# Shifted rows of a depthwise convolution copied inside on-chip memory instead of through a scratch tensor in device memory

## The chip, the cores and the metric

One Trainium2 chip, all 8 of its cores, each running the same program on its own share of the tokens, with no exchange between cores. The metric is device time in microseconds (us) of the slowest core, less being better. A run of the kernel before is shown three times (below), and one further execution was profiled.

## The reference, cut to what matters

One decoder layer on x of (2, 8192, 1024) float32:

```python
x = x + 0.5 * swiglu(rmsnorm(x, ffn1_norm), w_gate, w_up, w_down)          # FFN 1, hidden 2816
h = rmsnorm(x, mix_norm)
glu_a, glu_b, q, k, v, g_conv, g_attn = split(h @ w_in)
u = glu_a * sigmoid(glu_b)                                                  # 1024 channels
c = causal_depthwise_conv(u, dw_w, dw_b)        # out[t] = sum_k w[k] * u[t - 30 + k], width 31
c = silu(layernorm(c)) @ conv_w_proj
a = sliding_window_gqa_sinks(rope(q), rope(k), v, sinks) @ attn_w_o         # window 128
x = x + (sigmoid(g_conv + b1) * c + sigmoid(g_attn + b2) * a) @ w_out
x = x + 0.5 * swiglu(rmsnorm(x, ffn2_norm), ...)                            # FFN 2
out = rmsnorm(x, final_norm)
```

The part that changes is how the gated inputs `u` get to the causal convolution: every output needs the 30 tokens in front of it.

## The kernel before, in words

Each core has 2048 tokens and a halo of 128 tokens in front, as four tiles of 512 tokens (NT). Channels lie on the 128 partitions, in 8 chunks, and tokens along the free dimension. A tile goes through FFN 1 (`f_a`), the mixer (`m_norm`, `m_rest`) and FFN 2 (`f_b`). The mixer of tile t is interleaved with FFN 2 of tile t-1 and FFN 1 of tile t+1, so that TensorE has FFN matmuls (`ps<-xnF,wt`, `ps<-Hh,wt`) to run between those of the mixer (`ps<-xnM,wt`).

The convolution stage of a tile stands at the start of `m_rest` (L854). For the 8 channel chunks cc, in a software pipeline: `glu(cc)` (L724) makes the gated chunk, `u_in(cc)` (L739) follows one step behind, `conv(cc)` (L746) three steps behind. `glu` runs two projections of 8 matmuls of 512 columns, a tanh on ACT (ScalarE), and one scalar_tensor_tensor on DVE (VectorE), which writes the tile `uT`, of three buffers. A DMA on the queue of SP (SyncE) then writes `uT` to the scratch tensor `ush` in device memory. `u_in` reads it back with 4 DMAs into `RR`, a tile of four buffers. `RR` has partition 32*k + c holding channel c shifted by k tokens, for k of 0 to 3, and the four groups g of 32 channels side by side. So `conv` contracts 4 taps at a time over the 128 partitions: 8 tap groups times 4 channel groups is 32 matmuls of a 128x32 weight and 512 columns (`ps<-RR,wt`), read at the free offset 4*j. A DVE tensor_scalar then moves the result to `cvo`. In tile 0 `glu` is also run over the 128 halo tokens (matmuls `ps<-S,wt` of 128 columns, the gated halo in a part of `S` named `uh`), and this goes to `ush` by a DMA of its own (`ush<-S`). In later tiles the 31 columns in front of a tile are in `ush` already.

Weights come through nine slots `wt`, shared by everything. The first read of a block is float32, from `wall` or `wd`, by a DMA on POOL's queue (GpSimd). The block is stored once as bf16 in `wac` or `wdc` (`wac<-wt`), and later reads are `wt<-wac` and `wt<-wdc`. The stores and the cached reads are issued on SP's queue, in between the DMAs of the convolution. SP issues in program order, and an instruction that waits for a semaphore holds back all that stands behind it.

What sets the order: `Plan.schedule` (L185) places the recorded tasks on the engines by estimated durations and by keys. `Plan.dma` (L178) gives a DMA task an estimated issue time of 0.1 us per DMA, and `t` as the time to landing. `Stream` (L230) decides when weight loads and stores are issued. Those estimates set only the order. The waits are made from true dependencies (`_deps`, L62): `u_in` waits for the writes of `ush` and, from the fifth chunk on, for the convolution that last read the same `RR` buffer. `glu` waits, for its `uT` buffer, for the DMA that last read it.

Helpers record every compute instruction, so most rows name L82 (`emit_op`), L98 (`emit_dma`) or L508 (`MMW`), and the tiles tell them apart.

Of the kernel before, what the change touches and what calls it, by code (L numbers as in the profile page):

```python
# [15 lines left out]
RW = 28 + NT  # L16
# [119 lines left out]
class Plan:  # L136
# [32 lines left out]
    def op(self, eng, fn, rd=(), wr=(), t=None, use=None):  # L169
        k = self._task(eng)  # L170
        k.ops.append((0, fn, tuple(rd), tuple(wr), use))
        k.t += eng.typ if t is None else t
        if use is not None and use not in k.uses:
            k.uses.append(use)
            use.left += 1
        self._link(k, rd, wr)

    def dma(self, q, dsem, moves, rd=(), wr=(), t=5.0):  # L178
        k = self._task(q)
        k.ops.append((1, dsem, tuple(rd), tuple(wr), moves))  # L180
# [168 lines left out]
def build_nc():  # L349
    nc = bass.Bass("TRN2", target_bir_lowering=False)  # L350
    dt = nc.dram_tensor
# [9 lines left out]
    outT_d = dt("outT", [D, TOK], F32, kind="ExternalOutput").ap()  # L361
    wac_d = dt("wac", [NBLK_A, 128, 2048], BF16, kind="Internal").ap()
    wdc_d = dt("wdc", [32, 128, 11 * 128], BF16, kind="Internal").ap()
    ush_d = dt("ush", [8, 128, TL], BF16, kind="Internal").ap()

    with ExitStack() as es:
        def sb(name, shape, dtype):
            return es.enter_context(nc.sbuf_tensor(name, shape, dtype))

        def mksem(name):  # L370
            return Sem(es.enter_context(nc.semaphore(name)))
# [12 lines left out]
        def bufs(n):  # L384
            return [Buf() for _ in range(n)]
# [3 lines left out]
        xnM = sb("xnM", [128, 8, NT], BF16); xnM_b = bufs(8)  # L389
# [3 lines left out]
        qa = sb("qa", [128, 8, NT], BF16); qa_b = [[Buf() for _ in range(4)] for _ in range(8)]  # L393
        kT = sb("kT", [128, 2, 640], BF16); kT_b = [[Buf(), Buf()] for _ in range(2)]
        V = sb("V", [128, 5, 256], BF16); V_b = bufs(5)
        uT = sb("uT", [128, 3, NT], BF16); uT_b = bufs(3)
        NRR = 4
        RR = [sb(f"RR{i}", [128, 4, RW], BF16) for i in range(NRR)]; RR_b = bufs(NRR)
        RR_s = [mksem(f"s_rr{i}") for i in range(NRR)]
        ush_b = bufs(8); ush_s = [mksem(f"s_ush{i}") for i in range(3)]  # L400
        NW = 9
        wt = [sb(f"wt{i}", [128, 2048], BF16) for i in range(NW)]; wt_b = bufs(NW)
        wt_s = [mksem(f"s_wt{i}") for i in range(NW)]
# [7 lines left out]
        S = sb("S", [128, 8, 132], F32); S_b = bufs(2)  # L411
# [16 lines left out]
        xnh = S[:].rearrange("p a b -> p (a b)")[:, 0:512].bitcast(BF16).rearrange("p (a b) -> p a b", a=8); xnh_b = bufs(8)  # L428
# [4 lines left out]
        s_x = [mksem(f"s_x{i}") for i in range(8)]  # L433
        s_xh = mksem("s_xh")
        s_pos = [mksem(f"s_pos{i}") for i in range(2)]
        ushh_b = bufs(8); ushh_s = [mksem(f"s_ushh{i}") for i in range(2)]
        uh = S[:].rearrange("p a b -> p (a b)")[:, 768:896].bitcast(BF16).rearrange("p (a b) -> p a b", a=2); uh_b = bufs(2)
        s_out = [mksem(f"s_out{i}") for i in range(8)]

        ps = [es.enter_context(nc.psum_tensor(f"ps{i}", [128, NT], F32)) for i in range(3)]  # L440
# [37 lines left out]
        SA = SD = Stream(chan, POOL, SP, wview, wt_b, wt_s, wt_ss, wt_hs, wsrc, wcache, [8.0] * 3 + [18.0 + 2.0 * i for i in range(NW - 3)],  # L478
                         {"A": (3.6, 1.6, 1.7), "D": (2.5, 1.1, 1.2), "W": (1.8, 0.8, 0.85)}, (X_b[0][5],))
        alias(cvo_b, Xh_b + Hhh_b + [accH[1]])  # L480
        alias(S_b, xnh_b + uh_b + [cosh_b, sinh_b])

        def ACTF(out, in_, func, rd, wr, t=None, **kw):
            op(ACT, partial(act, out=out, in_=in_, func=func, **kw), rd, wr, t)

        def STT(out, in0, scalar, in1, op0, op1, rd, wr, t=None):
            op(DVE, partial(stt, out=out, in0=in0, scalar=scalar, in1=in1, op0=op0, op1=op1), rd, wr, t)
# [13 lines left out]
        def COPY(out, in_, rd, wr, t=None):  # L501
            op(DVE, partial(nc.vector.tensor_copy, out=out, in_=in_), rd, wr, t)
# [4 lines left out]
        def MMW(out, use, pick, rhs, start, stop, rd, wr, t=None):  # L507
            op(PE, lambda: mm(out, lhsT=pick(use.slot), rhs=rhs, start=start, stop=stop), rd, wr, t, use)  # L508

        def load_x(t, after=()):  # L510
            b0 = HALO + t * NT
            for c in range(8):
                dma(ACT if t == 0 and c % 2 else SP, s_x[c], [(X[t % 2][:, c, :], xT_d[128 * c:128 * c + 128, b0:b0 + NT])],
                    rd=after, wr=(X_b[t % 2][c],), t=7.0)

        def proj(pst, pb, use, sub, rhs_t, rhs_bufs, N):
            G.join(True)
            for kc in range(8):
                MMW(pst[:, 0:N], use, lambda s, kc=kc: s[:, kc, sub * 128:(sub + 1) * 128], rhs_t[:, kc, 0:N], kc == 0, kc == 7,
                    rhs_bufs[kc] if isinstance(rhs_bufs[kc], list) else [rhs_bufs[kc]], (pb,), t=N / 2360)  # L520
            G.join(False)

# [566 lines left out]
```

How the kernel before makes its waits and increments, by code:

```python
    def wait(self, sem, val):  # L40
        if val <= 0:
            return
        if sem is self.sem:
            if val > sem.n or not SAME_ENGINE_SYNC or self.no_self:
                return
        if self.known.get(sem, 0) >= val:
            return
        self.e.wait_ge(sem.h, val)
        self.known[sem] = val
# [29 lines left out]
def emit_op(eng, fn, rd=(), wr=()):  # L79
    for s, v in _deps(rd, wr, eng.sem).items():
        eng.wait(s, v)
    inst = fn()
    eng.sem.n += 1
    inst.then_inc(eng.sem.h, 1)
    ev = eng.sem.n
    for b in wr:
        b.w = {eng.sem: ev}
        b.r = {}
    for b in rd:
        if b.r.get(eng.sem, 0) < ev:
            b.r[eng.sem] = ev
# [1 line left out]
def emit_dma(q, dsem, moves, rd=(), wr=()):  # L93
    for s, v in _deps(rd, wr, None).items():
        q.wait(s, v)
    q.wait(dsem, dsem.n)
    for out_ap, in_ap in moves:
        q.e.dma_start(out=out_ap, in_=in_ap).then_inc(dsem.h, 16)
        dsem.n += 16
    for b in wr:
        b.w = {dsem: dsem.n}
        b.r = {}
    for b in rd:
        b.r[dsem] = dsem.n
```

## Time and profile before

| what | us |
|---|---|
| three runs | 1957.9, 1786.03, 1765.64 (median 1786.03) |
| the profiled execution's own time | 1768.82 |
| its span, from first to last instruction (slowest core, core 5) | 1767.8 |
| spans of the 8 cores | 1748.8 to 1767.8 |
| TensorE (PE) busy | 1638.3 (93% of the span) |
| VectorE (DVE), ScalarE (ACT), GpSimd (POOL) busy | 704.0, 651.8, 687.7 |

How to read it: busy is time in which the engine ran an instruction. PE is matmuls, PEld the loading of weights into the array. Queue rows (SPq) are the issuing of DMAs and are not counted as busy. In a timeline row the first number is the start and the second the duration of a merged run of x instructions; what stands in brackets is how long the engine idled before it, and what ended that. The granted clock is TensorE's, as a share of full speed.

### The profile page before, as it was taken

Reading aid. Unit: us, or ns where it says so; the run is one execution under the profiler, and the core shown is the slowest. Engines: PE = TensorE matmul, PEld = TensorE weight load, DVE = VectorE, ACT = ScalarE, POOL = GpSimd, SP = SyncE. Lnnn points to the kernel's source line nnn. Section 1 sums busy time; section 2 is a strip of 40 time slices with the busy share of each in tenths; the row PEclk is TensorE's granted clock in tenths of the full one; section 3 lists DMA queues with packets and bytes.
Section 4 is the critical chain, followed back from the end, with each engine's and each line's share of the span. In section 5 each row is a group of like instructions: output and inputs, shape, how many; then the busy total and the mean of one; then the engine's idle time right before and its main releaser. Section 6 shows DMA issues by size and latency. Waiting matters only on the chain.

```text
span 1767.8 us, 29593 instructions; the slowest of 8 cores (1748.8 to 1767.8 us)
## 1 busy us (share of the span) xinstructions
PE 1638.3 (93%) x9060; PEld 739.0 (42%) x9060; DVE 704.0 (40%) x1180; ACT 651.8 (37%) x1396; POOL 687.7 (39%) x723
## 2 busy tenths in 40 slices
PE   6999677899988899989999999999998999998996
PEld 2555333344433334434443344444443444443442
DVE  3432422764243365441225266542224356524212
ACT  3212312664132366443222257553222258422221
POOL 1014023865332595413331387423322277413232
PEclk9999788999999999999999999999999999999998
DMA  8998987579999999985556978764443953443542
GB/s 171 197 217 167 208 204 178 140 190 183 203 196 239 233 180 172 192 274 156 163 147 176 238 198 190 194 240 152 142 138 115 237 199 98 145 152 128 182 123 81
DMA packets 118121, 315.39 MB, mean 178 GB/s; under 512 B 14544, under 2 KB 36304, under 8 KB 117968
## 3 DMA queue, kind: packets, MB, share of 16 engines
q1 hardware_dynamic: 92480, 231.46, 41.8%
q0 software_dynamic: 24768, 80.95, 29.0%
q8 instruction: 78, 1.28, 0.3%
q10 hardware_dynamic: 720, 1.09, 0.2%
q14 instruction: 75, 0.61, 0.1%
HBM read 327.01 MB, written 67.37 MB: 223 GB/s over the span
## 4 chain that ended last, share of the span: by engine, by line
PE 80%; DMA 11%; issue 2%; ACT 2%; DVE 2%; SPq 2%; POOL 1%; ACTq 0%; DVEq 0%; POOLq 0%
PE ps L508 74%; PE ps L82 5%; DMA RR<-ush 3%; DMA ush<-S 3%; DMA ush<-uT 2%; SPq L98 2%; DMA X<-xT 1%; DMA wt<-wall 1%; PE ps L706 1%; DMA outT<-tf 1%; ACT ps L82 0%; POOL acc L82 0%; DVE xnF L82 0%; DVE S L82 0%; ACT S L82 0%
## 5 line engine op out<-in xcount | busy, mean ns | idle before, releaser
L508 PE MATMUL ps<-xnF,wt 128*128 128x512 bf16 x2816 | 652.1, 386 | 15.9 <-DVE xnF L82 6.5
L508 PEld LDWEIGHTS ps<-xnF,wt 128*128 128x128 bf16 x2816 | 270.0, 99 | 357.2 <-issue 64.3
L508 PE MATMUL ps<-Hh,wt 128*128 128x512 bf16 x1408 | 328.6, 380 | 0.0
L508 PE MATMUL ps<-xnM,wt 128*128 128x512 bf16 x1344 | 310.9, 383 | 0.4 <-DVE xnM L82 0.2
L82 ACT ACTIVATE tf<-ps 128x512 f32<-128x512 f32 x304 | 179.9, 595 | 312.5 <-PE ps L508 291.0
L82 POOL TENSOR_TENSOR Hh<-tf 128x512 bf16<-128x512 f32 x128 | 164.7, 1287 | 187.9 <-PE ps L508 115.1
L82 DVE SCALAR_TENSOR_TENSOR tf<-tf,ps 128x512 f32<-128x512 f32 x176 | 120.4, 684 | 260.8 <-PE ps L508 248.0
L508 PEld LDWEIGHTS ps<-Hh,wt 128*128 128x128 bf16 x1408 | 134.3, 98 | 160.8 <-issue 9.3
L508 PEld LDWEIGHTS ps<-xnM,wt 128*128 128x128 bf16 x1344 | 129.9, 98 | 169.7 <-issue 22.2
L98 POOL DMA_DIRECT2D wt<-wall x121 | 67.7, 563 | 245.6 <-PE ps L508 214.5
L82 DVE SCALAR_TENSOR_TENSOR X<-ps,X 128x512 f32<-128x512 f32 x96 | 66.3, 691 | 199.5 <-PE ps L508 197.5
L82 ACT ACTIVATE S<-S,sm 128x129 f32<-128x129 f32 x256 | 103.6, 405 | 65.8 <-DVE sm L82 47.5
L82 DVE SCALAR_TENSOR_TENSOR tm<-tm,ps 128x512 f32<-128x512 f32 (+1 forms) x86 | 50.2, 585 | 168.9 <-PE ps L508 150.1
L508 PE MATMUL ps<-RR,wt 128*32 128x512 bf16 x1024 | 72.2, 431 | 40.9 <-DMA RR<-ush 40.8
L82 POOL TENSOR_TENSOR acc<-acc,tf 128x512 f32<-128x512 f32 x56 | 70.9, 1266 | 91.5 <-ACT tf L82 91.3
L82 POOL TENSOR_TENSOR cvo<-tm 128x512 bf16<-128x512 f32 x32 | 40.5, 1265 | 157.0 <-DVE tm L82 157.0
L508 PE MATMUL ps<-cvo,wt 128*128 128x512 bf16 (+1 forms) x432 | 97.0, 314 | 0.8 <-POOL cvo L82 0.8
L82 POOL TENSOR_TENSOR acc<-acc,tm 128x512 f32<-128x512 f32 x56 | 70.8, 1264 | 66.4 <-ACT tm L82 66.1
L82 POOL TENSOR_TENSOR P<-S,sm 128x512 bf16<-128x512 f32 x64 | 67.3, 1051 | 68.7 <-DVE sm L82 24.5
L82 POOL TENSOR_TENSOR cvo<-cvo,acc 128x512 f32<-128x512 f32 x64 | 83.4, 1307 | 14.6 <-ACT acc L82 13.3
L82 ACT ACTIVATE tm<-cvo 128x512 f32<-128x512 f32 (+1 forms) x67 | 39.7, 595 | 133.2 <-DVE cvo L82 131.5
L82 ACT ACTIVATE tm<-ps,hcols_sb 128x512 f32<-128x512 f32 x64 | 43.6, 688 | 113.3 <-PE ps L508 108.4
(97 smaller groups left out, 1471.8 us busy)
## 6 DMA issues: line engine op xcount, KB each, us to landing
wt<-wac SPq DMA_DIRECT2D x207, 512.0 KB, 4.8
wt<-wall POOLq DMA_DIRECT2D x121, 512.0 KB, 9.7
wac<-wt SPq DMA_DIRECT2D x82, 512.0 KB, 8.7
wt<-wdc SPq DMA_DIRECT2D x80, 352.0 KB, 3.1
RR<-ush SPq DMA_DIRECT2D x128, 135.0 KB, 6.3
wt<-wd POOLq DMA_DIRECT2D x48, 352.0 KB, 7.1
wdc<-wt SPq DMA_DIRECT2D x32, 352.0 KB, 5.8
X<-xT SPq DMA_DIRECT2D x28, 256.0 KB, 10.8
```

Source lines behind the costliest of these rows:

```text
L82: inst = fn()
L98: q.e.dma_start(out=out_ap, in_=in_ap).then_inc(dsem.h, 16)
L508: op(PE, lambda: mm(out, lhsT=pick(use.slot), rhs=rhs, start=start, stop=stop), rd, wr, t, use)
L706: op(PE, lambda kc=kc: mm(pst[:, 0:256], lhsT=xn_t[:, kc, c0:c0 + 128], rhs=uv.slot[:, kc, 0:256], start=(kc == 0), stop=(kc == 7)), (xn_b ...
```

## The change

The gated chunk no longer goes to device memory. `uT` grows to 32 + 512 columns: columns 0 to 30 are the 31 tokens in front of the tile, 31 to 542 the tile's own. In tile 0 the front columns come from a `glu` over the last 31 halo tokens alone (matmuls of 31 columns instead of 128). In later tiles a DVE copy brings them from a new tile `past`, and every `glu` ends with a DVE copy that saves its last 31 columns there. `u_in` is now 16 DMAs instead of 4, one for each pair of shift k and channel group g, each from 32 partitions of `uT` to 32 partitions of `RR`. The tensor `ush`, its buffers and its semaphores, and the `uh` part of `S` are gone. The plan's estimate of issue time is 0.35 us per DMA for tasks of 8 and more DMAs.

```diff
@@ class Plan, dma
-        k.t = 0.1 * len(moves)
+        k.t = (0.1 if len(moves) < 8 else 0.35) * len(moves)
@@ build_nc
-    ush_d = dt("ush", [8, 128, TL], BF16, kind="Internal").ap()
...
-        uT = sb("uT", [128, 3, NT], BF16); uT_b = bufs(3)
+        uT = sb("uT", [128, 3, 32 + NT], BF16); uT_b = bufs(3)
+        past = sb("past", [128, 8, 32], BF16); past_b = bufs(8)
...
-        ush_b = bufs(8); ush_s = [mksem(f"s_ush{i}") for i in range(3)]
...
-        def proj(pst, pb, use, sub, rhs_t, rhs_bufs, N):
+        def proj(pst, pb, use, sub, rhs_t, rhs_bufs, N, c0=0):
             G.join(True)
             for kc in range(8):
-                MMW(pst[:, 0:N], use, lambda s, kc=kc: s[:, kc, sub * 128:(sub + 1) * 128], rhs_t[:, kc, 0:N], kc == 0, kc == 7,
+                MMW(pst[:, 0:N], use, lambda s, kc=kc: s[:, kc, sub * 128:(sub + 1) * 128], rhs_t[:, kc, c0:c0 + N], kc == 0, kc == 7,
...
         def glu(cc, base, halo):
             use = SA.use(("A", 28 + cc), "M")
-            parts = [(xnM, xnM_b, NT, uT[:, cc % 3, :], uT_b[cc % 3], base, ush_s[cc % 3], ush_b[cc])]
+            u_t, u_b = uT[:, cc % 3, :], uT_b[cc % 3]
+            parts = [(xnM, xnM_b, 0, NT, u_t[:, 31:31 + NT])]
             if halo:
-                parts.append((xnh, xnh_b, HALO, uh[:, cc % 2, :], uh_b[cc % 2], 0, ushh_s[cc % 2], ushh_b[cc]))
-            for xn_t, xn_bufs, N, u_t, u_b, c0, sem, db in parts:
+                parts.append((xnh, xnh_b, HALO - 31, 31, u_t[:, 0:31]))
+            else:
+                COPY(u_t[:, 0:31], past[:, cc, 0:31], (past_b[cc],), (u_b,), 0.15)
+            for xn_t, xn_bufs, c0, N, dst in parts:
...
-                STT(u_t, t_t[:, 0:N], 1.0, pa[:, 0:N], ALU.add, ALU.mult, (t_b, pab), (u_b,))
-                dma(SP, sem, [(ush_d[cc][:, c0:c0 + N], u_t)], rd=(u_b,), wr=(db,), t=6.0)
+                STT(dst, t_t[:, 0:N], 1.0, pa[:, 0:N], ALU.add, ALU.mult, (t_b, pab), (u_b,), t=0.15 + 0.55 * N / 512)
+            COPY(past[:, cc, 0:31], u_t[:, NT:NT + 31], (u_b,), (past_b[cc],), 0.15)
 
         def u_in(cc, base):
-            dma(SP, RR_s[cc % NRR], [(RR[cc % NRR][32 * k:32 * k + 32, :, :],
-                                      ush_d[cc][:, base - 31 + k:base - 31 + k + RW].rearrange("(g c) t -> c g t", g=4)) for k in range(4)],
-                rd=(ush_b[cc], ushh_b[cc]), wr=(RR_b[cc % NRR],), t=8.0)
+            dma(SP, RR_s[cc % NRR], [(RR[cc % NRR][32 * k:32 * k + 32, g, :], uT[32 * g:32 * g + 32, cc % 3, k:k + RW])
+                                     for k in range(4) for g in range(4)], rd=(uT_b[cc % 3],), wr=(RR_b[cc % NRR],), t=6.0)
```

SP's queue in the convolution stage of the last tile (tile 3), the first chunks, before the change. `ush<-uT` is the write of a gated chunk, `RR0<-ush ... x4` the read of its shifted rows, `wt<-wac` a cached weight load:

```order
L98 DMA ush<-uT 128x512
L98 DMA wt0<-wac 128x2048
L98 DMA wt7<-wac 128x2048
L98 DMA ush<-uT 128x512
L98 DMA wt8<-wac 128x2048
L98 DMA RR0<-ush 32x4x540 x4
L98 DMA ush<-uT 128x512
L98 DMA wt2<-wac 128x2048
L98 DMA RR1<-ush 32x4x540 x4
```

The same place after the change:

```order
L98 DMA RR0<-uT 32x540 x16
L98 DMA wt3<-wac 128x2048
L98 DMA RR1<-uT 32x540 x16
L98 DMA wt6<-wac 128x2048
L98 DMA wt4<-wac 128x2048
L98 DMA wt5<-wac 128x2048
L98 DMA RR2<-uT 32x540 x16
L98 DMA wt0<-wac 128x2048
L98 DMA RR3<-uT 32x540 x16
```

The write and the read of a chunk became one block of 16 DMAs, and each block stands as a whole ahead of the next weight load. Over the stage, 8 writes and 32 reads became 128 copies, with ten weight loads between the first block and the last.

TensorE's queue at the first convolution of tile 3, before. `ps<-xnM` with wt5 are the last of the gating projections of the first four chunks, `ps<-xnF` FFN matmuls, `ps<-RR0` the convolution of chunk 0:

```order
L508 MATMUL ps7<-xnM,wt5 128x512 x8
L508 MATMUL ps2<-xnF,wt6 128x512 x8
L508 MATMUL ps0<-xnF,wt4 128x512 x8
L508 MATMUL ps1<-xnF,wt4 128x512 x8
L508 MATMUL ps2<-xnF,wt0 128x512 x8
L508 MATMUL ps34<-RR0,wt7 32x512 x32
L508 MATMUL ps6<-xnM,wt8 128x512 x8
```

And after:

```order
L505 MATMUL ps7<-xnM,wt2 128x512 x8
L505 MATMUL ps2<-xnF,wt7 128x512 x8
L505 MATMUL ps0<-xnF,wt1 128x512 x8
L505 MATMUL ps34<-RR0,wt8 32x512 x32
L505 MATMUL ps6<-xnM,wt3 128x512 x8
```

Of the four groups of 8 FFN matmuls ahead of the first convolution two are left; the other two stand later, behind the stage. In tile 2 it is the same. In tile 1 the stage has as many FFN matmuls as before, and in tile 0 one group of 8 fewer.

## Rows read from the trace of the kernel before

**Rows 1.** The page: span, busy time of TensorE.

```profile
span 1767.8 us, 29593 instructions; the slowest of 8 cores (1748.8 to 1767.8 us)
PE 1638.3 (93%) x9060; PEld 739.0 (42%) x9060; DVE 704.0 (40%) x1180; ACT 651.8 (37%) x1396; POOL 687.7 (39%) x723
```

**Rows 2.** Waits of TensorE: who waited for whom, us in total, times, longest.

```profile
PE ps L508 <- DMA RR<-ush: 40.8, 11, 11.8
PE ps L508 <- DMA wt<-wac: 5.2, 1, 5.2
```

**Rows 3.** Busy time by stretch: the convolution stages of tiles 0 to 3.

```profile
core 5: us, PE busy (x) PEld busy (x) DVE busy (x) ACT busy (x) POOL busy (x), PEclk, DMA share, GB/s
183.00:293.00 110.00, 79.82 (x602) 37.01 (x601) 30.79 (x55) 22.12 (x38) 21.78 (x25) 0.84 0.92 209
530.00:600.00 70.00, 58.08 (x420) 24.15 (x421) 20.54 (x32) 13.64 (x22) 18.80 (x20) 0.90 0.97 234
959.00:1019.00 60.00, 56.69 (x433) 24.14 (x435) 20.23 (x31) 13.63 (x22) 15.69 (x14) 0.97 0.96 231
1364.00:1420.00 56.00, 54.94 (x425) 23.48 (x427) 19.56 (x30) 13.95 (x23) 16.21 (x13) 1.00 0.96 243
```

**Rows 4.** Timeline of TensorE, convolutions of tile 0: the third last and the last.

```profile
263.16 3.32 PE L508 MATMUL ps<-RR,wt 128*32 128x512 bf16 x32 [2.83 <-DMA RR<-ush]
...
289.83 3.60 PE L508 MATMUL ps<-RR,wt 128*32 128x512 bf16 x32 [11.79 <-DMA RR<-ush]
```

**Rows 5.** Timeline of SP's queue, tile 0.

```profile
190.27 0.32 SPq L98 DMA_DIRECT2D ush<-uT  x1
...
193.22 0.43 SPq L98 DMA_DIRECT2D ush<-S  x1
...
209.69 1.75 SPq L98 DMA_DIRECT2D RR<-ush  x4
```

**Rows 6.** Timeline of SP's queue: the first gated chunk of tiles 1, 2 and 3.

```profile
530.15 1.77 SPq L98 DMA_DIRECT2D ush<-uT  x2
...
959.26 0.32 SPq L98 DMA_DIRECT2D ush<-uT  x1
...
1364.28 0.32 SPq L98 DMA_DIRECT2D ush<-uT  x1
1364.74 0.82 SPq L98 DMA_DIRECT2D wt<-wac  x2
```

**Rows 7.** Timeline of TensorE: last convolutions of tiles 1 to 3, an FFN group before.

```profile
599.72 1.91 PE L508 MATMUL ps<-RR,wt 128*32 128x512 bf16 x32 [0.45 <-DMA RR<-ush]
...
1018.11 1.91 PE L508 MATMUL ps<-RR,wt 128*32 128x512 bf16 x32
...
1373.53 7.07 PE L508 MATMUL ps<-xnF,wt 128*128 128x512 bf16 x32
...
1419.52 1.91 PE L508 MATMUL ps<-RR,wt 128*32 128x512 bf16 x32
```

**Rows 8.** Timeline of SP's queue, tile 3: two of its eight groups of 4 reads.

```profile
1368.67 1.76 SPq L98 DMA_DIRECT2D RR<-ush  x4
...
1372.16 3.38 SPq L98 DMA_DIRECT2D RR<-ush  x4
```

**Rows 9.** Issues on SP's queue by kind: duration ns min/median/max.

```profile
L98 SPq DMA_DIRECT2D wt<-wac x207: 319/320/1626, 188.6 to 1683.1; - x104
L98 SPq DMA_DIRECT2D RR<-ush x128: 302/429/1958, 209.7 to 1413.3; - x128
L98 SPq DMA_DIRECT2D cvo<-xT x1: 942/942/942, 5.1 to 5.1; - x1
```

**Rows 10.** Reads of tile 3 (RR<-ush, 1360 to 1420): from issue to landing.

```profile
DMA to landing us min/median/max: 3.2/6.1/9.7
```

**Rows 11.** Groups by line and shape: halo matmuls, a small DVE instruction.

```profile
L508 PE MATMUL ps<-S,wt 128*128 128x128 bf16 x496 | 33.1, 219 | 1.2 <-ACT tm L82 1.2
L82 DVE RECIPROCAL sm<-sm 128x4 f32<-128x4 f32 x64 | 11.0, 172 | 31.9 <-ACT S L82 31.7
```

More of the change, by code:

```diff
@@ L435, in build_nc @@
         s_pos = [mksem(f"s_pos{i}") for i in range(2)]
-        ushh_b = bufs(8); ushh_s = [mksem(f"s_ushh{i}") for i in range(2)]
-        uh = S[:].rearrange("p a b -> p (a b)")[:, 768:896].bitcast(BF16).rearrange("p (a b) -> p a b", a=2); uh_b = bufs(2)
         s_out = [mksem(f"s_out{i}") for i in range(8)]
@@ L480, in build_nc @@
         alias(cvo_b, Xh_b + Hhh_b + [accH[1]])
-        alias(S_b, xnh_b + uh_b + [cosh_b, sinh_b])
+        alias(S_b, xnh_b + [cosh_b, sinh_b])
         def ACTF(out, in_, func, rd, wr, t=None, **kw):
@@ L725, in glu @@
             use = SA.use(("A", 28 + cc), "M")
-            parts = [(xnM, xnM_b, NT, uT[:, cc % 3, :], uT_b[cc % 3], base, ush_s[cc % 3], ush_b[cc])]
+            u_t, u_b = uT[:, cc % 3, :], uT_b[cc % 3]
+            parts = [(xnM, xnM_b, 0, NT, u_t[:, 31:31 + NT])]
             if halo:
-                parts.append((xnh, xnh_b, HALO, uh[:, cc % 2, :], uh_b[cc % 2], 0, ushh_s[cc % 2], ushh_b[cc]))
-            for xn_t, xn_bufs, N, u_t, u_b, c0, sem, db in parts:
+                parts.append((xnh, xnh_b, HALO - 31, 31, u_t[:, 0:31]))
+            else:
+                COPY(u_t[:, 0:31], past[:, cc, 0:31], (past_b[cc],), (u_b,), 0.15)
+            for xn_t, xn_bufs, c0, N, dst in parts:
                 pa, pab = bM5.get()
                 pb_, pbb = bM5.get()
-                proj(pb_, pbb, use, 1, xn_t, xn_bufs, N)
+                proj(pb_, pbb, use, 1, xn_t, xn_bufs, N, c0)
                 t_t, t_b = tmM.get()
-                ACTF(t_t[:, 0:N], pb_[:, 0:N], AF.Tanh, (pbb,), (t_b,), scale=0.5)
-                proj(pa, pab, use, 0, xn_t, xn_bufs, N)
-                STT(u_t, t_t[:, 0:N], 1.0, pa[:, 0:N], ALU.add, ALU.mult, (t_b, pab), (u_b,))
-                dma(SP, sem, [(ush_d[cc][:, c0:c0 + N], u_t)], rd=(u_b,), wr=(db,), t=6.0)
+                ACTF(t_t[:, 0:N], pb_[:, 0:N], AF.Tanh, (pbb,), (t_b,), t=0.2 + 0.4 * N / 512, scale=0.5)
+                proj(pa, pab, use, 0, xn_t, xn_bufs, N, c0)
+                STT(dst, t_t[:, 0:N], 1.0, pa[:, 0:N], ALU.add, ALU.mult, (t_b, pab), (u_b,), t=0.15 + 0.55 * N / 512)
+            COPY(past[:, cc, 0:31], u_t[:, NT:NT + 31], (u_b,), (past_b[cc],), 0.15)
         def u_in(cc, base):
-            dma(SP, RR_s[cc % NRR], [(RR[cc % NRR][32 * k:32 * k + 32, :, :],
-                                      ush_d[cc][:, base - 31 + k:base - 31 + k + RW].rearrange("(g c) t -> c g t", g=4)) for k in range(4)],
-                rd=(ush_b[cc], ushh_b[cc]), wr=(RR_b[cc % NRR],), t=8.0)
+            dma(SP, RR_s[cc % NRR], [(RR[cc % NRR][32 * k:32 * k + 32, g, :], uT[32 * g:32 * g + 32, cc % 3, k:k + RW])
+                                     for k in range(4) for g in range(4)], rd=(uT_b[cc % 3],), wr=(RR_b[cc % NRR],), t=6.0)
         taps = [None]
```

## The prediction

> **What bounds the kernel now.** I read the page first: TensorE is busy 1638.3 of 1767.8 us [rows 1]. The kernel is bound by it, so an edit counts only through the 129.5 us in which TensorE stands, or by making it stand more. Then TensorE's waits: the largest is for the shifted rows, 40.8 us in 11 waits, and one wait of 5.2 us for a cached weight load [rows 2]. Then the four convolution stages one by one [rows 3]: TensorE is busy 79.8 of 110 us in tile 0, 58.1 of 70 in tile 1, 56.7 of 60 in tile 2 and 54.9 of 56 in tile 3. So the wait to be removed sits almost wholly in the first two tiles. In tiles 2 and 3 there is next to nothing to win. Behind a long wait TensorE also runs slower for a few us: the 32 matmuls of a convolution take 1.91 us at full clock and 3.3 to 3.6 behind waits of 2.8 and 11.8 us [rows 4, 7], and the granted clock of the stage is 0.84 in tile 0 against 1.00 in tile 3 [rows 3]. That is some 1.7 us for each of the seven or so long waits, 12 us. All that could be won is thus 40.8 + 5.2 + 12 = 58 us.
>
> **Why it waits.** The path of a chunk is: gating on DVE, write to `ush`, landing, read into `RR`, landing, convolution. SP stands at the wait for the write before it may issue the read, with everything behind it: in tile 0 the halo write goes out at 193.2 and the reads only at 209.7 [rows 5]. The change takes out one of the two landings and this stop.
>
> **What it adds.** SP now issues 128 copies of 34.6 KB (32 partitions x 540 x 2 bytes) per tile, in blocks of 16, in place of 8 writes and 32 reads (in tile 0 also 8 halo writes). The trace has no copy of 32 partitions and none within on-chip memory, so its issue is bounded from both sides. Low end: a load behind a pause takes 0.32 us [rows 9], 16 of them 5.1. High end: the eight groups of 4 reads of tile 3 take 16.7 us together, from about 1.7 to 3.38 each (two of the eight in [rows 8]), which is 0.52 per read and 8.3 per block. Between them lies the plain group of 4 in 1.76 us, 0.44 each, 7.0 for 16. This is the nearest row, since such a read, too, goes to blocks of 32 partitions in rows of 540 elements, and 429 ns is the median of all 128 [rows 9]. I take it. With 0.14 us of waiting in front of a block (0.46 from one issue to the next less 0.32 for the issue itself [rows 6]) a block is 7.2 us.
>
> The Trainium skill, page "DMA: Bandwidth & Descriptors", section "Why a DMA increments its semaphore by 16 and not by 1", gives a plain copy 512 cycles of the issuing sequencer in the older generation, data transfer not counted. At the 1.2 GHz of the SyncEngine ("Trainium Kernel Development and Optimization", NeuronCore Architecture) that is an estimate of 0.43 us whatever the size, and speaks against four times as many DMAs. By it a block would be 6.9 us; a cost that shrank with the size would bring it to the low end. The 429 ns of the reads agree with it, the 320 ns of loads behind a pause do not.
>
> **Does SP keep up?** While TensorE runs densely, a chunk is 16 gating matmuls and one convolution. 32 FFN matmuls take 7.07 us [rows 7], so 16 take 3.5, and with 1.9 that makes 5.4 us per chunk, against 7.2 plus the weight loads on SP. The queue of SP therefore becomes what sets the end of the stage. That end is when the last convolution starts: first gated chunk, plus 8 x 7.2 = 57.6, plus the other issues between the blocks at 0.46 each, plus the last landing. A read of tile 3 lands after 3.2 us at least and 6.1 in the median [rows 10], under bursts of four 138 KB reads; I take 4.5.
> - Tile 3: first chunk 1364.3 [rows 6]. Ten weight loads, 4.6. 1364.3 + 57.6 + 4.6 + 4.5 = 1431.0. Before it was 1419.5 [rows 7]; 16 FFN matmuls fewer stand ahead of it, so like is compared with 1416.0. Loss 15.0.
> - Tile 2: 959.3 + 57.6 + 5.1 (eleven issues) + 4.5 = 1026.5, against 1018.1 - 3.5 = 1014.6. Loss 11.9.
> - Tile 1: 530.2 + 57.6 + 5.1 + 4.5 = 597.4 against 599.7 [rows 7]. Gain 2.3.
> - Tile 0: the chunk is written at 190.3 [rows 5], with its front columns at about 192. 192 + 57.6 + 3.7 + 6.1 (the median landing, as this is the stage full of float32 weight loads) = 259.4, against 289.8 [rows 4] less 1.8 for 8 FFN matmuls. That would be 28.6 won. The DMA engines are 92% busy there for 110 us [rows 3], 101 us of work, of which only the writes, some 4 us, go. Weights loaded ahead give slack, but hardly 28 us; I take 20, with 12 and 28 as ends.
>
> Sum: 15.0 + 11.9 - 2.3 - 20 = +4.6 us on the profiled execution's 1768.8: 1773 us. (The median of the three runs shown, 1786, lies 17 above that execution and their lowest 3 below; I forecast on the scale of the profiled one.)
>
> **Small terms.** The 56 new DVE copies of 31 columns cost about as much as the smallest DVE instruction, 0.17 us [rows 11]: 14 in a tile, 2.4 us, while DVE is busy only 20 of 60 us of a stage [rows 3]; hidden. If DVE were full they would cost 9.6 us in all. The copy into `uT` waits until the block of three chunks earlier has landed, and behind it on DVE stand the gating, the moving of a finished convolution to `cvo` and the FFN's products, which free TensorE's banks. The convolution next on TensorE waits for the same landing, so I put it at 0, with at most 1.4 us (two DVE instructions) on each of 16 chunks, 22 us, as the other end. The halo's 128 matmuls shrink from 128 to 31 columns: at 33.1 us for 496 [rows 11] all of them are 8.5 us and at most 6.5 could go; SP paces tile 0, so 0. Weight loads behind a block go out up to 7 us later; they are planned ahead, 0.
>
> **The rivals.**
> 1. Issue is cheap: 0.32 us per copy, a block of 5.3. Then SP keeps pace with TensorE. Tile 3 comes out even, tile 2 wins its waits (3), tile 1 its 12 and one slow restart (13), tile 0 28: 44 us, 1725 us. For it: every load behind a pause, and the first read of a group, takes this. Against: reads in a row don't. Half way, at 0.37, it is 28 us, 1741.
> 2. Slower: SP's queue is held up as it was between the reads. The place is the 128 back-to-back issues of each tile, the price 0.52 per copy, 8.5 us per block, 10.4 us more per tile. Tile 3 loses 25.4, tile 2 22.3, tile 1 8.1, and tile 0 wins 12: +44, 1813 us. One us on a block is worth 8 us in each of four tiles, 32, so the time passes 2% (35 us) from a block of 8.2 us, 0.50 per copy. For it: 3.38 us for four reads in the quietest tile [rows 8]. Against: a block spreads the same bytes over 7 us instead of under 2, which leaves the queues emptier.
> 3. The landing of float32 weights holds SP in tile 0, so the one tile that should win gives only 4 us: 1789.
>
> **How the numbers follow.** A measurement of this kernel can tell about 2% from no change. Forecast 0.52 (1750 to 1800). Rival 1 0.20, of which 0.13 lies beyond 2% (under 1733) and the rest between 0.32 and 0.37 per copy. Rival 2 0.23. Rival 3 0.05. So faster 0.13, same 0.64, slower 0.23. The range takes in the cheap issue almost to its end and all of rival 2: 1728 to 1818.
>
> **What would show it.** Right: SP's row for the new copies has a median near 0.43 us and blocks of about 7 us; TensorE's waits for `RR` shrink in tile 0, stay in tile 1, and appear in tiles 2 and 3 as a series of short waits of 2 us, with the last convolution of tile 3 about 67 us behind the first gated chunk. Wrong: a median of 0.32 and blocks under 6 us; or waits of TensorE that name DVE or `wt`; or tile 0 with as long a stage as before.

## Result, and the profile after

The changed kernel took 1880.04, 1881.23 and 1962.45 us (median 1881.23) against a median of 1786.03 before: a ratio of 1.061 [1.053, 1.068], slower by 6%. Some executions, of either kernel, show a lower granted clock on the cores of one die and take longer (1962.45 here, 1957.9 before); ratios, and the medians of the kernel before that stand under Experiments, leave them out. The profiled execution took 1880.04 us, against 1768.82. The forecast was 1773, range 1728 to 1818; the result lies outside it, on the side of the second rival.

The page of the kernel after (slowest core, core 6): the span, the busy times, the chain of work that ended last by engine, the costliest group of the convolution (count | busy us, mean ns | idle before it and its releaser), and the row of the new copies among the DMA issues (count, KB each, median us from issue to landing).

```profile
span 1879.0 us, 29979 instructions; the slowest of 8 cores (1860.7 to 1879.0 us)
...
PE 1662.0 (88%) x9060; PEld 743.5 (40%) x9060; DVE 710.0 (38%) x1236; ACT 650.3 (35%) x1396; POOL 689.5 (37%) x723
...
PE 70%; SPq 17%; DMA 5%; issue 3%; DVE 2%; ACT 2%; POOL 1%; ACTq 0%; DVEq 0%; POOLq 0%
...
L505 PE MATMUL ps<-RR,wt 128*32 128x512 bf16 x1024 | 94.8, 535 | 126.2 <-DMA RR<-uT 95.9
...
RR<-uT SPq DMA_DIRECT2D x512, 33.8 KB, 2.3
```

The same three rows of the kernel before, the chain, the convolution and the DMA that fills `RR`:

```profile
PE 80%; DMA 11%; issue 2%; ACT 2%; DVE 2%; SPq 2%; POOL 1%; ACTq 0%; DVEq 0%; POOLq 0%
L508 PE MATMUL ps<-RR,wt 128*32 128x512 bf16 x1024 | 72.2, 431 | 40.9 <-DMA RR<-ush 40.8
RR<-ush SPq DMA_DIRECT2D x128, 135.0 KB, 6.3
```

The span grew by 111.2 us. TensorE's busy time grew by 23.7 of them [rows 1], though it runs fewer columns: the 1024 convolution matmuls take 535 ns each in place of 431. The rest is idle time, 217.0 us against 129.5. A sixth of the chain (17%, before 2%) is now SP's queue, that is, an engine that computes nothing. The copies themselves are quick: from issue to landing 2.3 us in the median.

TensorE's waits after (us in total, times, longest), and SP's issues (duration in ns, least/median/most; first and last start):

```profile
PE ps L505 <- DMA RR<-uT: 95.9, 20, 8.2
...
PE ps L505 <- DVE uT L82: 30.2, 7, 7.0
...
PE ps L505 <- DMA wt<-wac: 4.0, 5, 2.3
```

```profile
L98 SPq DMA_DIRECT2D RR<-uT x512: 507/591/1966, 190.4 to 1525.0; - x171
L98 SPq DMA_DIRECT2D wt<-wac x207: 319/320/1100, 185.5 to 1794.1; - x104
```

The wait for the shifted rows, 40.8 us in 11 waits before [rows 2], is 95.9 in 20. And an issue of the new copies holds SP for 591 ns in the median and never under 507, where a read of `ush` took 429 [rows 9]. The loads of weights, on the same queue among them, still take 320.

The four convolution stages in windows (busy us of PE, PEld, DVE, ACT, POOL with the instruction counts, then the granted clock, the DMA engines' busy share, GB/s), to be held against [rows 3]:

```profile
183.00:288.00 105.00, 73.80 (x562) 31.70 (x565) 30.72 (x64) 20.67 (x37) 21.33 (x24) 0.82 0.76 176
535.00:631.00 96.00, 56.88 (x402) 22.91 (x399) 19.46 (x40) 12.42 (x20) 18.77 (x19) 0.80 0.67 170
985.00:1088.00 103.00, 72.09 (x471) 29.72 (x470) 28.72 (x57) 15.12 (x25) 16.09 (x14) 0.87 0.42 112
1434.00:1530.00 96.00, 66.01 (x442) 26.75 (x440) 22.00 (x43) 13.62 (x22) 16.20 (x13) 0.86 0.37 108
```

All four stages now look alike: from the first block to the start of the last convolution they take 92 to 101 us, where they took 55 to 100 before. TensorE's granted clock in them is 0.80 to 0.87. In tiles 2 and 3 the DMA engines are busy only 0.42 and 0.37 of the time (0.96 before), and TensorE waits all the same. What paces the stage is thus not the transfer. SP's timeline in the stage of tile 3 (start, duration; merged runs), with the first blocks of tiles 1 and 2 ahead of it, shows what does:

```profile
527.20 10.40 SPq L98 DMA_DIRECT2D RR<-uT  x16
...
992.16 10.30 SPq L98 DMA_DIRECT2D RR<-uT  x16
...
1435.29 10.99 SPq L98 DMA_DIRECT2D RR<-uT  x16
1446.43 0.48 SPq L98 DMA_DIRECT2D wt<-wac  x1
1447.05 10.23 SPq L98 DMA_DIRECT2D RR<-uT  x16
1457.42 1.43 SPq L98 DMA_DIRECT2D wt<-wac  x3
1459.00 10.15 SPq L98 DMA_DIRECT2D RR<-uT  x16
...
1514.98 10.60 SPq L98 DMA_DIRECT2D RR<-uT  x16
```

The queue has no gap: block, weight loads, block. A block takes 10.0 to 11.1 us, the eight together 83.3, so 10.4 each; within a block one copy follows the other by 0.63 us in the median. Three last convolutions, those of tiles 0 to 2, and then three convolutions of tile 3 (in brackets the idle time before, and its releaser):

```profile
287.61 1.91 PE L505 MATMUL ps<-RR,wt 128*32 128x512 bf16 x32
...
628.01 3.60 PE L505 MATMUL ps<-RR,wt 128*32 128x512 bf16 x32 [8.00 <-DMA RR<-uT]
...
1084.23 3.28 PE L505 MATMUL ps<-RR,wt 128*32 128x512 bf16 x32 [3.63 <-DMA RR<-uT]
...
1458.80 3.36 PE L505 MATMUL ps<-RR,wt 128*32 128x512 bf16 x32 [4.98 <-DMA RR<-uT]
...
1470.76 3.60 PE L505 MATMUL ps<-RR,wt 128*32 128x512 bf16 x32 [4.84 <-DVE uT L82]
...
1527.00 3.60 PE L505 MATMUL ps<-RR,wt 128*32 128x512 bf16 x32 [5.39 <-DMA RR<-uT]
```

A convolution starts 1 to 2 us behind the end of its block (block 1459.00 to 1469.15, convolution 1470.76; last block to 1525.58, convolution 1527.00). Before it TensorE has idled for 3.6 to 5.4 us in five of the eight chunks of tile 3, and behind that idling its 32 matmuls take 3.1 to 3.6 us in place of 1.91, little more than half the rate. Over the four tiles 22 of the 32 convolutions are slow in this way, against 7 before. That is the 22.6 us by which the convolution's busy time grew (94.8 against 72.2).

Some of these waits are put down to a DVE copy. DVE at that time:

```profile
1470.50 0.18 DVE L82 COPY uT<-past 128x31 bf16<-128x31 bf16 x1 [7.42 <-DMA RR<-uT]
1470.78 0.69 DVE L82 SCALAR_TENSOR_TENSOR uT<-tm,ps 128x512 bf16<-128x512 f32 x1
```

That copy had itself been waiting for a landing, began at 1470.50 and ended 0.08 us before the convolution. In tile 3 the two convolutions whose wait names DVE start 1.6 and 1.7 us behind the end of their block, the other six 1.4 to 1.8. So the copy is not the cause but work of a second engine that the same landing lets go.

### The profile page after: what moved, and what is told of

It is laid out like the page before. It is cut to its first block, busy times and chain, and to the rows that moved or that the text cites. A ratio compares the mean times of both kernels' runs of the same rounds, so it can differ in the third digit from the quotient of the medians.

```text
span 1879.0 us, 29979 instructions; the slowest of 8 cores (1860.7 to 1879.0 us)
## 1 busy us (share of the span) xinstructions
PE 1662.0 (88%) x9060; PEld 743.5 (40%) x9060; DVE 710.0 (38%) x1236; ACT 650.3 (35%) x1396; POOL 689.5 (37%) x723
## 4 chain that ended last, share of the span: by engine, by line
PE 70%; SPq 17%; DMA 5%; issue 3%; DVE 2%; ACT 2%; POOL 1%; ACTq 0%; DVEq 0%; POOLq 0%
PE ps L505 64%; SPq L98 17%; PE ps L82 5%; DMA X<-xT 2%; DMA RR<-uT 1%; DMA outT<-tf 1%; PE ps L703 1%; DVE xnF L82 0%; ACT ps L82 0%; POOL acc L82 0%; DVE tf L82 0%; DVE tm L82 0%; ACT L82 0%; POOL P L82 0%; ACT sx L82 0%
## 5 line engine op out<-in xcount | busy, mean ns | idle before, releaser
L505 PE MATMUL ps<-RR,wt 128*32 128x512 bf16 x1024 | 94.8, 535 | 126.2 <-DMA RR<-uT 95.9
L82 ACT ACTIVATE tm<-cvo 128x512 f32<-128x512 f32 (+1 forms) x67 | 39.3, 592 | 218.0 <-DVE cvo L82 217.0
L505 PEld LDWEIGHTS ps<-RR,wt 128*32 128x32 bf16 x1024 | 35.6, 123 | 175.6 <-issue 168.5
L82 POOL TENSOR_TENSOR acc<-acc,cvo 128x512 f32<-128x512 f32 x24 | 30.4, 1265 | 192.9 <-DVE cvo L82 192.9
## 6 DMA issues: line engine op xcount, KB each, us to landing
RR<-uT SPq DMA_DIRECT2D x512, 33.8 KB, 2.3
```

The source lines that it names most:

```text
L82: inst = fn()
```

## Experiments

Two theories of the price of an issue stood against each other. A: an issue whose source is on the chip takes SP 0.59 us, whatever its size. B: it is the shape, 32 partitions and one row of 1080 bytes each, or the small size. The rest is about what follows from the price: is it SP's queue that sets the time, or the places that the plan's estimate gives the blocks; and would another engine or queue do the work for less? Where no median is given, the kernel ran once. The kernel before was run again beside them: its median was 1769.28 us beside the 16 reads from device memory, the copies over 128 partitions, the four copies and the split with ACT; 1768.08 beside the copies of 32 columns, the write in four, the estimate of 0.62 and the 16 copies on DVE; and 1770.66 beside the other four. The diffs are shortened, and `n` in them is `cc % NRR`.

### The kernel before, with 16 reads of the small shape

```diff
-  k.t = 0.1 * len(moves)
+  k.t = (0.1 if len(moves) < 8 else 0.35) * len(moves)
...
-  (RR[n][32*k:32*k+32, :, :], ush_d[cc][:, base-31+k:base-31+k+RW].rearrange("(g c) t -> c g t", g=4)) for k in range(4)
+  (RR[n][32*k:32*k+32, g, :], ush_d[cc][32*g:32*g+32, base-31+k:base-31+k+RW]) for k in range(4) for g in range(4)
```

> The kernel before, still through ush in device memory, but with the 16 reads of 32 partitions x 540 columns per chunk in place of 4, and the plan's 0.35 us for them. Theory A (a copy from on-chip memory to on-chip memory costs SP more than one from device memory): an issue stays near 0.43 us (median), a block of 16 near 7 us, and the time is some 1800 to 1830 us. Theory B (a copy of 32 partitions costs 0.59 us whatever its source, or the number is all that counts): median 0.59 us, blocks of 10 us, and the time is above the changed kernel's 1880, some 1900 us, as the landing of the write comes on top.

Measured: 1846.24 us. SP's issues and TensorE's waits:

```profile
L98 SPq DMA_DIRECT2D RR<-ush x512: 302/422/2006, 206.0 to 1504.5; - x171
```

```profile
PE ps L508 <- DMA RR<-ush: 43.2, 12, 9.5
PE ps L508 <- DMA wt<-wac: 36.5, 13, 6.2
```

The same number of copies of the same shape costs 422 ns each when the source is in device memory; the blocks of tile 3 take 7.3 to 8.7 us. So the shape is not what costs 591. But the time lies 16 us above the range expected under A: the count is dear even at 422 ns. With the write and its landing kept, 16 issues in place of 4 and the plan's 0.35 for them, this kernel is 77 us slower than before. TensorE idles 34.6 us more, most of it for weights (36.5 against 5.2), whose loads stand behind the blocks on the same queue, and is busy for 42.8 us more (1681.1 against 1638.3).

### 16 copies over all 128 partitions

```diff
-  (RR[n][32*k:32*k+32, g, :], uT[32*g:32*g+32, cc % 3, k:k+RW]) for k in range(4) for g in range(4)
+  (RR[n][:, g, 135*j:135*j+135], uT[:, cc % 3, 135*j:135*j+135]) for j in range(4) for g in range(4)
```

> The changed kernel with 16 copies of 128 partitions x 135 columns per chunk (same number, same bytes, on-chip to on-chip, but without the move across partitions, so the convolution reads unshifted data). Theory A (on-chip source is dear): median issue again 0.55 to 0.6 us and a time near 1880. Theory B (the 32-partition shape is dear): issue back at 0.43 us, blocks of 7 us, time near 1790 to 1810. More and shorter descriptors per copy could raise the issue on their own; then it is above 0.6.

Measured: 1892.44 us.

```profile
L98 SPq DMA_DIRECT2D RR<-uT x512: 464/601/4042, 187.8 to 1537.6; - x171
```

The same bytes over 128 partitions cost as much. B falls for the partitions. (This kernel leaves out the move across partitions, and is a measure of time only.)

### 16 copies of 32 columns

```diff
-  (RR[n][32*k:32*k+32, g, :], uT[32*g:32*g+32, cc % 3, k:k+RW])
+  (RR[n][32*k:32*k+32, g, 0:32], uT[32*g:32*g+32, cc % 3, k:k+32])
```

> The changed kernel with 16 copies of 32 partitions x 32 columns per chunk instead of 540 (it leaves out the other 508 columns; RR is set to 0 once at the start). If the issue of an on-chip copy costs a fixed time whatever its size: median again 0.59 us, blocks of 10 us, and the time is within 15 us of the changed kernel's 1880. If transfer, landing or queues that fill up hold the issue back: median under 0.45 us and a time under 1800.

Measured: 1879.08 us, with copies of 2.0 KB.

```profile
L98 SPq DMA_DIRECT2D RR<-uT x512: 507/591/1593, 189.2 to 1526.2; - x171
```

A seventeenth of the bytes changes neither the issue (591) nor the time (1880.04; the copies leave out 508 of 540 columns). The transfer has no part in the loss.

### The kernel before, its write to `ush` in four DMAs

```diff
-  (ush_d[cc][:, c0:c0+N], u_t)
+  (ush_d[cc][:, c0+i*N//4:c0+(i+1)*N//4], u_t[:, i*N//4:(i+1)*N//4]) for i in range(4)
```

> The kernel before with each write of a gated chunk to ush as 4 DMAs of 128 columns (on-chip to device memory), to see issues of that direction one behind the other. If it is the on-chip source that makes an issue dear, they take 0.59 us in a row; if it is that both ends lie on chip, they take 0.42 as the reads from device memory do. The time is 1770 to 1790 us either way (96 more issues, 40 to 60 us on SP, most of it under waits it has anyway).

Measured: 1774.59 us.

```profile
L98 SPq DMA_DIRECT2D ush<-uT x128: 319/434/4517, 191.1 to 1411.1; - x128
```

From the chip to device memory an issue costs 434 ns, back to back, with `uT` as the source. Theory A as first put, an on-chip source, is thus too wide: it is a source and a destination that are both on the chip.

### Four copies of 128 partitions and 540 columns

```diff
+  (RR[n][:, g, :], uT[:, cc % 3, g:g+RW]) for g in range(4)
```

> The changed kernel with 4 copies of 128 partitions x 540 columns per chunk, on-chip to on-chip (same bytes, a quarter of the copies; it leaves out the move across partitions, the shift is by g instead of k). If the number of issues on SP's queue is what costs 6 per cent: blocks of 2.5 us at most, waits of TensorE for RR under 15 us in all, and 1725 to 1750 us, below the kernel before. If on-chip to on-chip transfer or the DVE copies into uT are the cause, it stays above 1800.

Measured: 1721.72 us, the fastest of all runs and 3 below what was expected; issues of 464/586/2977 ns. TensorE's waits, and SP's timeline in tile 3:

```profile
PE ps L505 <- DVE uT L82: 9.1, 1, 9.1
PE ps L505 <- DMA RR<-uT: 7.1, 1, 7.1
```

```profile
1336.49 2.37 SPq L98 DMA_DIRECT2D RR<-uT  x4
1341.82 2.35 SPq L98 DMA_DIRECT2D RR<-uT  x4
```

The same bytes move within the chip and the price per issue is the same, but there are four issues to a chunk, 2.4 us. Now SP waits for TensorE (a block each 5.4 us, the pace that the prediction worked out for it), and the whole gain that the idea promised is there: 48 us below the kernel before. Taking out the scratch tensor is good; the 12 further issues to a chunk, with the places that the plan gives the blocks (it counts a block here as 0.4 us, and as 5.6 us with 16 copies), cost 158 us. No run parts the two at four copies. This arrangement does not place shift k and channel group g as the convolution needs them, so it is a measure and not a way out.

### Eight copies of 64 partitions

```diff
+  (RR[n][64*h:64*h+64, g, :], uT[64*h:64*h+64, cc % 3, g:g+RW]) for h in range(2) for g in range(4)
```

> The changed kernel with 8 copies of 64 partitions x 540 columns per chunk (same bytes, on-chip to on-chip, half the number; it leaves out the move across partitions). The plan gives 0.35 us per copy, as for 16. Each issue stays at 0.59 us and a block takes 5.0 us, which with the weight loads is just about TensorE's 5.4 us per chunk. If the count of issues times 0.63 us against TensorE's pace is the whole mechanism, the loss is gone at this point, not halved: 1720 to 1750 us, close to the 1722 of four copies. If it goes by the count alone, it is half way between four and sixteen, 1790 to 1810.

Measured: 1768.21 us; issues of 461/597/3048 ns, waits for `RR` 26.5 us in 8.

```profile
1366.63 4.94 SPq L98 DMA_DIRECT2D RR<-uT  x8
1371.72 0.48 SPq L98 DMA_DIRECT2D wt<-wac  x1
1372.35 4.95 SPq L98 DMA_DIRECT2D RR<-uT  x8
```

Of the 158 us between four and sixteen copies 46 are left at eight. Neither expectation was met. From the first block of tile 3 (1354.17) to the last (1397.45) a chunk takes 6.2 us on SP, weight loads included, against TensorE's 5.4. Eight copies stand just beyond the point where SP's queue becomes the bound, so most of the loss is gone and some is left. This kernel too leaves out the move across partitions.

### The plan's estimate at the measured price

```diff
-  k.t = (0.1 if len(moves) < 8 else 0.35) * len(moves)
+  k.t = (0.1 if len(moves) < 8 else 0.62) * len(moves)
```

> The changed kernel with the plan's estimate for a task of 16 copies raised from 0.35 to 0.62 us each, the distance that the trace of the changed kernel shows; nothing else. If the damage came only from convolutions standing too early in TensorE's order, the plan now puts FFN matmuls between them: waits for RR fall below 40 us and the time to 1770 to 1810 us, with SP's blocks still 10 us long. If SP's queue is the bound in itself (it also carries the weight loads), the waits only move to weights and to the end of the stage: 1840 to 1880.

Measured: median 1850.91, ratio 1.043 [1.040, 1.045].

```profile
PE ps L505 <- DMA wt<-wac: 48.5, 16, 7.3
...
PE ps L505 <- DMA RR<-uT: 14.8, 4, 7.3
```

With the true price in the plan, TensorE waits little for `RR`, and for weights in its place: a load that stands behind a block comes late. The order is worth some 30 us. The remaining 4% goes with the queue: in tile 3 SP has no gap here either, with blocks of 9.8 to 10.7 us and 21 weight loads between the first and the last, 12.0 us per chunk.

### The plan's estimate at 0.1 for every DMA

```diff
+  k.t = 0.1 * len(moves)
```

> The changed kernel with the plan's old estimate, 0.1 us per DMA, for the 16 copies too; nothing else. Convolutions then stand as close behind one another as before. If SP's queue is the bound, their wait only grows by what FFN work is taken out from between: 1875 to 1910 us. If the order that 0.35 us gives was itself a part of the loss, it is under 1860.

Measured: 1934.18 us; waits for `RR` 93.9 us in 17, and 54.4 in 10 that name the DVE copy. The worse the estimate, the later the work: 0.62 gives 1851, 0.35 gives 1880, 0.1 gives 1934. The last, a single run, lies 24 us above what was expected, so the order matters more than I had put it at.

### Half of the copies on ACT's queue

```diff
-  k.t = (0.1 if len(moves) < 8 else 0.35) * len(moves)
+  k.t = (0.1 if len(moves) < 8 else 0.6) * len(moves)
...
-  dma(SP, RR_s[n], [... for k in range(4) for g in range(4)], ...)
+  for q, sems, bufs_, ks in ((SP, RR_s, RR_b, (0, 1)), (ACT, RR_s2, RR_b2, (2, 3))):
+      dma(q, sems[n], [... for k in ks for g in range(4)], ...)
```

> The changed kernel with the 16 copies of a chunk split: shifts 0 and 1 issued by SP, shifts 2 and 3 by ACT, each with its own semaphores; the plan gives 0.6 us per copy. The result is the reference's. If SP's queue is the bound: 8 issues take 5 us, less than TensorE's 5.4 us per chunk, waits for RR shrink to under 30 us and the time falls to 1745 to 1790 us. ACT gets 8 x 8 x 4 issues of 0.6 us, 154 us, and if it delays the tanh and the exponentials behind it, 1790 to 1830. If the issue is slow because both queues share one descriptor generator, each issue becomes about 1.2 us and nothing is won: 1870 to 1890.

Measured: median 1762.0, ratio 0.995 [0.990, 0.999].

```profile
L98 SPq DMA_DIRECT2D RR<-uT x256: 507/598/2401, 190.2 to 1397.3; - x128
L98 ACTq DMA_DIRECT2D RR<-uT x256: 514/619/2252, 193.6 to 1395.7; - x128
```

Both queues pay the price, and it does not double, as the third case of the expectation had it: they issue side by side, SP's at 598 ns against 591 alone. TensorE's waits for `RR` fall to 10.2 us in 5 (and 11.4 in 3 that name the DVE copy). Half the issues on each queue, with 0.6 in the plan, bring back the 6%, and not more. The estimate alone gave 1851 above, so the second queue is worth some 89 us of the 118.

### The 16 copies on DVE

```diff
-  k.t = (0.1 if len(moves) < 8 else 0.35) * len(moves)
+  k.t = (0.1 if len(moves) < 8 else 0.62) * len(moves)
...
-  dma(SP, RR_s[n], [...])
+  for k in range(4):
+      for g in range(4):
+          COPY(RR[n][32*k:32*k+32, g, :], uT[32*g:32*g+32, cc % 3, k:k+RW], (uT_b[cc % 3],), (RR_b3[n][4*k+g],), 0.25)
```

> The 16 copies of a chunk made by DVE (32 partitions x 540 columns, from one block of 32 partitions to another) instead of by DMA; SP issues none of them and there is no landing. The result is the reference's. If such a copy costs 0.2 to 0.3 us (bf16, in on-chip memory): DVE gets 512 of them, 100 to 150 us more, still under 60% busy, the waits of TensorE in the stages all but go, and the time is 1715 to 1745 us, as with four copies. If it costs 0.55 us or more, as DVE's float32 instructions of 512 columns do, a stage needs 70 us of DVE for the copies alone beside 20 for the rest, and the time is over 1820.

Measured: median 1799.73, ratio 1.020 [1.014, 1.026]. The costliest group of the page, DVE's timeline, POOL's, and a window of tile 3 (columns as above):

```profile
L82 DVE COPY RR<-uT 32x540 bf16<-32x540 bf16 x512 | 191.7, 374 | 15.1
```

```profile
1390.96 5.16 DVE L82 COPY RR<-uT 32x540 bf16<-32x540 bf16 x16
...
1398.00 7.08 DVE L82 COPY RR<-uT 32x540 bf16<-32x540 bf16 x16
```

```profile
1398.35 1.39 POOL L82 TENSOR_TENSOR acc<-cvo 128x512 f32<-128x512 f32 x1 [43.85 <-PE ps L506]
1399.69 1.32 POOL L82 TENSOR_TENSOR acc<-acc,tm 128x512 f32<-128x512 f32 x1
```

```profile
1385.00:1442.00 57.00, 41.30 (x323) 16.58 (x324) 52.35 (x128) 10.13 (x17) 13.26 (x11) 0.88 0.25 84
```

Half the copies take under 0.3 us (median 294 ns), but the mean is 374. The block beside no POOL work takes 5.16 us, the one beside two tensor_tensors 7.08. Of all 512 copies 40 took over 1 us, 1.25 to 1.79, and each of the 40 overlapped a POOL tensor_tensor and ended 0.15 to 0.17 us behind its end; of the 468 under 0.4 us only 18 touched one, by 0.25 us at most. The Trainium skill, page "SBUF — State Buffer", section "SBUF: two separate sides", says that GpSimd and VectorE, where VectorE runs in a two-port mode or has two inputs in on-chip memory, take one shared pair of ports as an exclusive lock for the whole instruction. These rows agree with it; in which mode the copies ran no run shows. The expectation had two cases, about 0.25 and 0.55 and more, and both missed: at a mean of 0.37 DVE is busy 52.35 of 57 us of tile 3's stage and takes SP's place as the bound.

### Half on DVE, half on SP

Shifts 0 and 2 by eight DVE copies, shifts 1 and 3 by eight DMAs of SP.

```diff
-  k.t = (0.1 if len(moves) < 8 else 0.35) * len(moves)
+  k.t = (0.1 if len(moves) < 8 else 0.62) * len(moves)
...
+  for k in (0, 2):
+      for g in range(4):
+          COPY(RR[n][32*k:32*k+32, g, :], uT[32*g:32*g+32, cc % 3, k:k+RW], (uT_b[cc % 3],), (RR_b3[n][4*k+g],), 0.38)
+  dma(SP, RR_s[n], [... for k in (1, 3) for g in range(4)], ...)
```

> The changed kernel with shifts 0 and 2 of each chunk copied by DVE (8 copies, 0.38 us each in the plan) and shifts 1 and 3 by 8 DMAs on SP (0.62 us each in the plan). The result is the reference's. Neither engine should then need more than TensorE's 5.4 us per chunk: SP 5.0 plus the weight loads, DVE 8 x 0.29 to 0.37 = 2.3 to 3 beside its 2 us. If the bound is whichever engine makes the copies, the time falls below both the changed kernel and the kernel before, 1725 to 1755 us. If the wait of DVE's copies and SP's issues on one another (both wait for the convolution that last read the buffer) adds up, 1760 to 1790.

Measured: median 1748.19, ratio 0.986 [0.981, 0.990]. This is below both kernels: 7% under the changed one, and 1.4% under the one before, clear of the interval but less than 2%.

```profile
PE ps L506 <- DMA RR<-uT: 13.3, 2, 11.8
...
PE ps L506 <- DVE RR L82: 10.3, 5, 5.1
...
PE ps L506 <- DMA wt<-wac: 5.5, 1, 5.5
```

Waits of 29 us are left of the 130 of the changed kernel.

### DVE, SP and ACT

Shifts 0 and 2 by DVE, shift 1 by four DMAs of SP, shift 3 by four of ACT.

```diff
-  k.t = (0.1 if len(moves) < 8 else 0.35) * len(moves)
+  k.t = (0.1 if len(moves) < 4 else 0.62) * len(moves)
...
+  for q, sems, bufs_, k in ((SP, RR_s, RR_b, 1), (ACT, RR_s2, RR_b2, 3)):
+      dma(q, sems[n], [... for g in range(4)], ...)
```

> As the run before it, with shift 1 issued by SP (4 DMAs) and shift 3 by ACT (4 DMAs). SP's block is 2.5 us, and ACT gets 4 x 0.62 = 2.5 us per chunk. If SP's queue still sets the pace with 8 issues, this gains another 10 to 20 us: 1715 to 1740 us. If it does not, it is the same or, through ACT's waits in front of its DMAs, 5 to 15 us slower than the run before it.

Measured: median 1739.75, ratio 0.982 [0.976, 0.987].

```profile
PE ps L507 <- DVE RR L82: 14.4, 7, 3.4
```

No wait for a DMA of shifted rows is left. It is 8 us below the version before it, where 10 to 20 had been expected; the intervals overlap, so which of the two is better stays open. Both, planned with 0.62, show that the idea of the change pays once its 16 issues are spread, and the 1721.72 of four copies says what is left in it.

## Why the prediction was wrong

**What bounds the kernel now.** Held, and with it what follows for the gain: the waits and the slow restarts behind them could win 58 us at most, and the kernel of four copies, which leaves out the shift across partitions, won 48.

**Why it waits.** Held: the landing is shorter (2.3 us in the median against 6.3 before, for a quarter of the bytes; 3.7 for the same 135 KB in the kernel of four copies), and the stop of SP for the write is gone.

**What it adds: here it failed.** The step "High end: ... 0.52 per read and 8.3 per block", and with it the 0.44 that I took between the ends. An issue takes 0.59, one follows another by 0.63, and a block takes 10.4. Every row that the two ends were made from was a DMA with one end in device memory, and the text said that the trace has none within on-chip memory; yet I let the dearest of the known kind stand as the end for the unknown kind. The runs put the difference where it is: 422 ns from device memory, 434 to device memory, 591 between two places on the chip, and 586 to 601 there whatever the size and the partitions. The Trainium skill's 512 cycles for a copy (page "DMA: Bandwidth & Descriptors", section "Why a DMA increments its semaphore by 16 and not by 1"), by the prediction's estimate 0.43 us, fit the first two and not the third; the measurement decides, and the figure's agreement with the 429 ns of the reads had lent the wrong figure weight.

**Does SP keep up?** Held, and its formula too. Putting 10.4 for 7.04 into it adds 27 us per tile:

| | forecast | with 27 more | measured |
|---|---|---|---|
| tile 3 | loss 15.0 | 42 | 40.0 |
| tile 2 | loss 11.9 | 39 | 36.7 |
| tile 1 | gain 2.3 | loss 25 | loss 31.2 |
| tile 0 | gain 20 (formula 28.6) | 2 gained | 0.5 gained |
| sum | +4.6 | +104 | +107.4 |

Measured is the length from the first chunk to the start of the last convolution, after less before: 91.7 less 55.2 in tile 3, 92.1 less 58.9 in tile 2, 100.8 less 69.6 in tile 1, 97.2 less 99.6 in tile 0 ([rows 4 to 7] and the rows above), with the 3.5, 3.5 and 1.8 us of FFN matmuls that no longer stand inside the stages added. 107.4 of the 111.2 us are in these four places. The sum of 104 takes the formula's 28.6 for tile 0; with the 20 that the forecast put there it is 112. Two smaller terms were off the other way from one another, which was luck: in tile 3 what stands between the blocks took 7.0 us and not 5.7, and from the end of the last block to the convolution it was 1.4 us and not 4.5.

**Small terms.** Held. The DVE copies of 31 columns take 0.18 us; what waits behind the copy into `uT` costs at most some tenths of a us (1.6 and 1.7 us behind the block against 1.4 to 1.8); DVE is busy 22.0 of 96 us. The weight loads behind a block cost 4.0 us of waits (5.2 before), but that goes by the plan: with 0.62 they cost 48.5. Landings of float32 weights in tile 0, rival 3, set nothing that shows: the blocks take 88.5 of that stage's 97.2 us by themselves.

**The rivals.** Rival 2 named the mechanism and the place rightly; its point from which the time passes 2% (0.50 per copy) no run tests. Its price of 0.52 was too small for the same reason as the forecast's. One us on a block was to be worth 32 us; 3.4 us came to 107. The time hung on one price that no row showed, at 32 us per us of a block, and the range took its upper end from rows of another kind. A price half above the nearest row (0.66, a block of 10.6) would have given some 1886 as its end.

**How the time would show.** The signs listed there read as follows: the median of the issue row 0.59 and not 0.43, waits as a series in tiles 2 and 3 as said, but mostly of 3.6 to 5.6 us in place of 2, and the last convolution of tile 3 92 us behind the first chunk, not 67. The idle time ahead of the convolutions did not shrink in tile 0 (28.1 us against 24.6) and did not stay in tile 1 (39.1 against 11.9). Two signs of being wrong came up: tile 0 takes as long as before (97.2 us against 99.6), and waits name DVE, though those lead back to the same landing.

## What to carry to other kernels

Price an edit that multiplies DMAs by issues x price against the pace of the engine that eats the data: here 16 x 0.63 us per chunk against TensorE's 5.4, while the DMA engines were busy 0.37 of the time in the last tile. Where an operation's kind is absent from the trace, the dearest known kind is not an upper bound; widen by the slope of the sum. Small copies to shifted partitions are best spread over two DMA queues and an engine with room, which here turned 6% slower into 0.5 to 1.8% faster. And give the planner the price that was measured.

## What the runs showed that I had not expected

- The issue of a DMA with both ends on the chip took 575 to 601 ns in the median on SP (619 on ACT in one run, 614 in another) and 461 to 507 at least. In the changed kernel 507 to 513 is the price of nearly every first copy of a block, and 591 the median of those behind it. With one end in device memory it took 422 to 434 and 302 to 319 at least. For 2.0, 33.8, 67.5 and 135 KB, and for 32, 64 and 128 partitions, it stayed within this range. What makes the difference no run shows.
- SP and ACT issued such copies side by side at 598 and 619 ns, against 591 for SP alone; ACT alone was not measured.
- A DVE copy of 32x540 bf16 to another block of partitions took 0.29 us, half of what an issue costs, and 1.25 to 1.79 when it met a tensor_tensor of POOL.
- After 2.8 to 8.2 us of idling, 22 of the 32 convolutions of the changed kernel took 3.0 to 3.6 us for their 32 matmuls; the other ten, behind 3.0 us or less, took 1.91. This made a fifth of the loss (22.6 of 111.2 us).
